# Second attention of a two-block kernel: one scan and differences ahead, masked heads in pairs

## The chip, the cores and the metric

The kernel runs on one core of one Trainium2 chip. The metric is device time in microseconds (us), the median of the runs shown. The engines are named as in the profile: PE is TensorE (PEld its weight loads), DVE is VectorE, ACT is ScalarE, POOL is GpSimd, SP is SyncE.

## The reference

256 tokens of width 1024 pass through two blocks. Each block is an attention part followed by an expert part in which all 16384 experts are computed densely (a product with `u`, a GELU and gate, a product with `v`). What is changed lies in the second block's attention part, which projects the normed tokens with `w_in_2` to seven groups of columns and computes two things from them.

The masked heads (8 heads of width 64, one key block of 256, so only the own block counts):

```python
s_own = einsum('hqd,hkd->hqk', q * hd**-0.5, k) - slopes[:, None, None] * dist
s_own = where(kpos <= tpos, s_own, -inf)
p = softmax(s_own, axis=-1)
o = einsum('hqk,hkd->qhd', p, v)
```

The recurrence (4 heads of width 128), which in closed form over the sequence is

```python
f = lb + (1 - lb) * sigmoid(f_pre);  kk = 1 - f;  cum = cumsum(log(f))
scores[t, s] = sum_d silu(q)[t, d] * exp(cum[t, d] - cum[s, d]) * kk[s, d]   # s <= t
o = scores @ i;  o = rmsnorm(o) * norm_g * silu(g)
```

The two results are concatenated and projected with `w_out_2`, then added to the residual.

## The kernel before, in words

All weights stream through a ring of four slots of 128x1024 (`ring`). SP loads a slot, ACT rounds it to `whi` (`highs_to`, L1206), POOL subtracts to get the rest `wlo` (L560, one instruction per slot), and PE multiplies with three products per pair of tiles, high times high, low times high, high times low (L626 to L628). PE's release of a slot (`slot_used`) lets ACT round the next one, so ACT and POOL must run in step with PE.

The second attention goes through 14 units of 256 columns (`IN2_SLOTS`: fr, fr, qr, qr, qa, ka, va, qa, ka, va, ir, ir, gr, gr). A unit is two ring slots and 48 products. The order of everything around the units is a list written out by `schedule2()`; PE, ACT and DVE each walk the same list in their `attention2()` and do their own share of each item. Every engine executes in order, so an item that waits holds back all that stands behind it in that engine's queue.

The recurrence works on levels: level 0 is the diagonal, level l (1 to 7) takes pairs of positions in blocks of 2^l, level 8 is the part between the two halves of 128. For each level DVE subtracts a column of the running sums from its block (`rec_decay`, L1865), ACT takes two exponentials (L1363, L1364), DVE multiplies them into the queries and keys (`rec_factors`, L1887 and L1888), PE forms the products (`rec_level`, L915) and DVE takes the wanted part of them (`rec_take`, L1875). The running sums come from eight scans of 128 elements, four after unit 2 and four after unit 3 (`rec_sums`, L1857). `LEVEL_AT` puts level l in unit 4 + l. Before the unit come that level's difference, the take of the level below and that level's factors; after it comes the level itself. So difference, exponentials, take and factors of a level all lie within one unit's time.

The masked heads run one at a time through scores on PE (L890, L891: 64 rows of the array), scale, mask and maxima on DVE (L1842 to L1844), exponentials on ACT (L1339), a reciprocal on DVE (L1847), scaling on ACT (L1345), three transposes on PE (L898), a copy on ACT (L1351), the product with the values on PE (L867, L868: 64 columns of the array), and the split of the result on ACT (L1354) and DVE (L1835). `SCORES_AT` gives the unit of each head's scores; its transposes come one unit later and its values two. `ml` and `mpT` hold two heads each, and so does `stat`. Even and odd heads lie in partitions 0 to 63 and 64 to 127, as `rows(h)` says.

The lines quoted here are those whose waits the prediction follows:

```python
pe.wait_ge(g_qk, i)                       # rec_level: factors of the level
pe.wait_ge(g_sc, TT * (i - 1) + t + 1)    # rec_level: the bank was taken
pe.wait_ge(m_prob, TT * (i + 1))          # m_turn: scaled probabilities
eng.wait_ge(g_exp, i)                     # rec_factors: exponentials
```

Of the kernel before, what the change touches and what calls it, by code (L numbers as in the profile page):

```python
# [21 lines left out]
P = 128  # L22
# [9 lines left out]
S = 256  # L32
TT = S // P
# [113 lines left out]
SCORES_AT = (6, 7, 8, 9, 9, 10, 10, 11)  # L147
LEVEL_AT = (4, 5, 6, 7, 8, 9, 10, 11, 12)


def schedule2():

    steps = []
    for s in range(len(IN2_SLOTS)):

        def heads(late):
            return [h for h in range(HEADS) if SCORES_AT[h] + late == s]

        levels = [l for l in range(9) if LEVEL_AT[l] == s]
        for l in levels:  # L160
            steps.append(("rec_decay", l))
        for h in heads(1):
            steps.append(("m_norm", h))
        for l in levels:
            if l:
                steps.extend([("rec_take", l - 1), ("rec_factors", l)])
        if 8 in levels:
            steps.append(("proj_half", s))
            steps.append(("rec_level", 8))
        if s == len(IN2_SLOTS) - 1:  # L170
            steps.append(("rec_norm", 0))
            steps.append(("proj_half", s))
            for h in heads(2):
# [4 lines left out]
        if s in (2, 3):  # L178
            steps.append(("rec_sums", s - 2))
        for l in levels:  # L180
            if l < 8:
                steps.append(("rec_level", l))
        if s == 12:
            steps.append(("rec_values", 0))
        for j in range(2):
            for h in heads(1)[j:j + 1]:
                steps.append(("m_turn", h))
            for h in heads(0)[j:j + 1]:
                steps.append(("m_scores", h))
            if s < len(IN2_SLOTS) - 1:  # L190
                for h in heads(2)[j:j + 1]:
                    steps.append(("m_values", h))
    steps.append(("rec_gate", 0))
    return steps


def block_program(nc, weights, const1, const2, gains, keys_in, x, out):
    with ExitStack() as ctx:
# [144 lines left out]
        rt, at = carve(at, TT, REC_H, P)  # L343
        lbs = work[:, 4608:4608 + 8 * REC_H].rearrange("p (k h) -> p k h", k=8)
# [9 lines left out]
        ones2 = c2[:, o:o + P]  # L354
# [16 lines left out]

        def mstat(h, k, t):

            return stat[:, 4, (h % 2) * 6 + 2 * k + t:(h % 2) * 6 + 2 * k + t + 1]

        def mstat2(h, k):
            return stat[:, 4, (h % 2) * 6 + 2 * k:(h % 2) * 6 + 2 * k + 2]
# [211 lines left out]
        def _(pe):  # L589
# [270 lines left out]
            def head_values(i):  # L860

                pe.wait_ge(m_Tc, i + 1)
                pe.wait_ge(proj_copied, base2 + 1 + i // 4)
                if i >= 2:
                    pe.wait_ge(m_outc, i - 1)
                w, v = mpT[:, i % 2, :], raw2["va"][:, :, i * HD:(i + 1) * HD]
                pe.matmul(ps[rows(i), 2, 0:S], v[:, 0, :], w[:, 0:S], start=True, stop=False, skip_group_check=True)  # L867
                pe.matmul(ps[rows(i), 2, P:S], v[:, 1, :], w[:, S:S + P], start=False, stop=True,  # L868
                          skip_group_check=True).then_inc(m_out, 1)

            def attention2():
                for what, i in schedule2():
# [10 lines left out]
                    elif what == "m_scores":  # L883
                        if i % 4 == 0:
                            pe.wait_ge(col_copied, 6 + i // 2)
                        if i >= 2:
                            pe.wait_ge(m_max, i - 1)
                        q, kT = colT["qa"][rows(i), i // 2, :], colT["ka"][rows(i), i // 2, :]
                        z = Z_BANK[i % 2]
                        pe.matmul(bank(z, 0, P), q[:, 0:P], kT[:, 0:P], start=True, stop=True)  # L890
                        pe.matmul(bank(z, P, P + S), q[:, P:S], kT, start=True, stop=True).then_inc(m_ready, 1)  # L891
                    elif what == "m_turn":
                        pe.wait_ge(m_prob, TT * (i + 1))
                        if i:
                            pe.wait_ge(m_Tc, i)
                        p = ml[:, i % 2, :]
                        for c in range(3):
                            mm = pe.transpose(bank(1, c * P, (c + 1) * P), p[:, c * P:(c + 1) * P], ident[:, :])  # L898
                        mm.then_inc(m_T, 1)
                    elif what == "m_values":  # L900
                        head_values(i)
# [37 lines left out]
                def heads_ready(kc):  # L939
                    pe.wait_ge(m_outc, 2 * kc + 4)  # L940
# [226 lines left out]
        def _(eng):  # L1167
# [139 lines left out]
            def attention2():  # L1307
                base = FIRST_GATE
                for what, i in schedule2():
# [25 lines left out]
                    elif what == "m_scores":  # L1335
                        eng.wait_ge(m_max, i + 1)
                        for t in range(TT):
                            c = slice(0, P) if t == 0 else slice(P, P + S)
                            eng.activation(ml[:, i % 2, c], ml[:, i % 2, c], ACT.Exp, bias=mstat(i, 0, t),  # L1339
                                           accum_out=mstat(i, 1, t)).then_inc(m_exp, 1)  # L1340
                    elif what == "m_norm":
                        eng.wait_ge(m_rec, i + 1)
                        for t in range(TT):
                            c = slice(0, P) if t == 0 else slice(P, P + S)
                            eng.activation(ml[:, i % 2, c], ml[:, i % 2, c], ACT.Copy, scale=mstat(i, 2, t)).then_inc(m_prob, 1)  # L1345
                    elif what == "m_turn":
                        eng.wait_ge(m_T, i + 1)
                        if i >= 2:
                            eng.wait_ge(m_out, i - 1)

                        eng.activation(mpT[:, i % 2, :], bank(1, 0, 384), ACT.Copy).then_inc(m_Tc, 1)  # L1351
                    elif what == "m_values":
                        eng.wait_ge(m_out, i + 1)
                        eng.activation(chi[rows(i), i // 2, :], ps[rows(i), 2, 0:S], ACT.Copy).then_inc(c_hi, 1)  # L1354
# [4 lines left out]
                    elif what == "rec_decay" and i:  # L1359
# [210 lines left out]
        def _(eng):  # L1570
# [251 lines left out]
            def attention2():  # L1822
                base = FIRST_GATE
                R = scale_row.unsqueeze(1).to_broadcast([P, 2, S])
                for what, i in schedule2():
# [7 lines left out]
                    elif what == "m_values":  # L1833
                        eng.wait_ge(c_hi, i + 1)
                        eng.tensor_tensor(clo[rows(i), i // 2, :], ps[rows(i), 2, 0:S], chi[rows(i), i // 2, :].bitcast(F32),  # L1835
                                          ALU.subtract).then_inc(m_outc, 1)
                    elif what == "m_scores":
                        l = ml[:, i % 2, :]
                        eng.wait_ge(m_ready, i + 1)
                        if i >= 2:  # L1840
                            eng.wait_ge(m_T, i - 1)
                        settle(eng.scalar_tensor_tensor(l, bank(Z_BANK[i % 2], 0, 384), HD ** -0.5, c2a[:, i, :], ALU.mult, ALU.add))  # L1842
                        eng.tensor_reduce(mstat(i, 0, 0), l[:, 0:P], AX.X, ALU.max, negate=True)
                        eng.tensor_reduce(mstat(i, 0, 1), l[:, P:P + S], AX.X, ALU.max, negate=True).then_inc(m_max, 1)  # L1844
                    elif what == "m_norm":
                        eng.wait_ge(m_exp, TT * (i + 1))
                        eng.reciprocal(mstat2(i, 2), mstat2(i, 1)).then_inc(m_rec, 1)  # L1847
# [5 lines left out]
                    elif what == "rec_sums":  # L1853
                        eng.wait_ge(g_log, 1)
                        for h in (2 * i, 2 * i + 1):
                            for t in range(TT):
                                tick(eng.tensor_tensor_scan(cum[:, h, t, :], ones2, dlt[:, h, t, :], 0.0, ALU.mult, ALU.add))  # L1857
                        eng.wait_ge(dve_step, steps[0])
                    elif what == "rec_decay" and i:
# [71 lines left out]
            def experts(b):  # L1931
# [132 lines left out]
                if b == 0:  # L2064
# [163 lines left out]
```

## Time and profile before

| What | Value |
| --- | --- |
| Median of 3 runs | 2045.97 us (2045.52 to 2046.14) |
| The profiled execution's own time | 2046.68 us |
| Its span | 2044.9 us |
| DVE, ACT, POOL busy | 61%, 50%, 69% of the span |

The span is the stretch between first and last instruction of the profiled execution; about 1.8 us of its own time lie around it. The second attention's units run from about 1076 to 1201 us of the span. Times on a timeline are counted from the span's start. The duration of a PE instruction includes its way through the array, so in a stream the distance from start to start, not the duration, is what each costs. The line number in a row is that of the kernel before.

### The profile page before, as it was taken

How to read it: one execution, taken by the hardware profiler on the slowest of the kernel's cores; microseconds unless marked ns; L12 is line 12 of the kernel's file. 1: busy time of each engine (PE TensorE's matmuls, PEld its weight loads, DVE VectorE, ACT ScalarE, POOL GpSimd, SP SyncE). 2: the span in 40 equal slices, each digit the busy share in tenths (PEclk: the TensorE clock that was granted, in tenths of full speed). 3: DMA queues.
4: the chain of work that ended last, by engine and by line, in shares of the span. 5: the costliest groups of instructions: out<-in, count | busy, mean ns of one | idle time of the engine just before them, and what ended most of it. 6: DMA issues, size and time to landing. Idle time of an engine off the chain costs nothing.

```text
span 2044.9 us, 39515 instructions
## 1 busy us (share of the span) xinstructions
PE 2022.4 (99%) x14308; PEld 1808.3 (88%) x14308; DVE 1247.5 (61%) x2142; ACT 1031.1 (50%) x1358; POOL 1418.0 (69%) x592
## 2 busy tenths in 40 slices
PE   8999999999999999999999999999999999999998
PEld 8999999999888888888889899999988888888886
DVE  5247469911676799953337537990376789994333
ACT  5557555454555544444446665545445554444443
POOL 6656868888777877754446456888877787775442
PEclk9999999999999999999999999999999999999999
DMA  7433545555545555565555334555555455555553
GB/s 257 154 125 125 174 158 181 178 182 184 173 168 174 175 174 169 170 224 184 192 187 175 104 121 149 185 184 184 176 174 174 168 173 173 174 169 180 185 186 132
DMA packets 97299, 351.46 MB, mean 172 GB/s; under 512 B 12112, under 2 KB 12368, under 8 KB 96848
## 3 DMA queue, kind: packets, MB, share of 16 engines
q1 hardware_dynamic: 96224, 345.40, 50.9%
q10 hardware_dynamic: 1008, 5.13, 0.7%
q8 instruction: 47, 0.77, 0.1%
q14 instruction: 20, 0.16, 0.0%
HBM read 349.44 MB, written 1.05 MB: 171 GB/s over the span
## 4 chain that ended last, share of the span: by engine, by line
PE 96%; DVE 2%; SPq 1%; DMA 0%; issue 0%; ACT 0%; POOL 0%; ACTq 0%; DVEq 0%
PE ps L626 24%; PE ps L628 23%; PE ps L627 23%; PE ps L1027 12%; PE ps L1028 6%; PE ps L1019 3%; PE ps L915 1%; PE ps L1003 1%; DVE act L1857 0%; SPq L536 0%; DMA ring<-in_weights 0%; PE ps L594 0%; DVE act L1865 0%; PE ps L815 0%; PE ps L795 0%
## 5 line engine op out<-in xcount | busy, mean ns | idle before, releaser
L560 POOL TENSOR_TENSOR wlo<-ring,whi 128x1024 fp32r<-128x1024 f32 x584 | 1410.1, 2419 | 594.1 <-ACT whi L1396 455.6
L1396 ACT ACTIVATE whi<-ring 128x1024 fp32r<-128x1024 f32 x536 | 566.4, 1060 | 774.9 <-PE ps L628 588.8
L626 PE MATMUL ps<-whi,shi 128*128 128x512 f32 x1024 | 408.5, 399 | 0.0
L628 PE MATMUL ps<-whi,slo 128*128 128x512 f32 x1024 | 405.9, 396 | 0.0
L627 PE MATMUL ps<-wlo,shi 128*128 128x512 f32 x1024 | 405.9, 396 | 0.0
L626 PE MATMUL ps<-hboth,whi 128*128 128x256 f32 x1392 | 395.7, 284 | 0.0
L627 PE MATMUL ps<-hboth,whi 128*128 128x256 f32 x1392 | 393.8, 283 | 0.0
L628 PE MATMUL ps<-hboth,wlo 128*128 128x256 f32 x1392 | 393.8, 283 | 0.0
L1027 PE MATMUL ps<-hboth,whi 128*128 128x512 f32 x1024 | 359.3, 396 | 0.0
L1028 PE MATMUL ps<-hboth,wlo 128*128 128x256 f32 x1024 | 283.7, 277 | 0.0
L626 PEld LDWEIGHTS ps<-hboth,whi 128*128 128x128 f32 x1392 | 267.1, 192 | 2.2 <-issue 2.0
L627 PEld LDWEIGHTS ps<-hboth,whi 128*128 128x128 f32 x1392 | 267.1, 192 | 0.0
L628 PEld LDWEIGHTS ps<-hboth,wlo 128*128 128x128 f32 x1392 | 267.1, 192 | 0.0
L628 PEld LDWEIGHTS ps<-whi,slo 128*128 128x128 f32 x1024 | 192.8, 188 | 46.8
L626 PEld LDWEIGHTS ps<-whi,shi 128*128 128x128 f32 x1024 | 192.9, 188 | 45.6
L627 PEld LDWEIGHTS ps<-wlo,shi 128*128 128x128 f32 x1024 | 193.0, 188 | 45.4
L1027 PEld LDWEIGHTS ps<-hboth,whi 128*128 128x128 f32 x1024 | 192.1, 188 | 43.0
L2038 DVE TENSOR_TENSOR wlo<-ring,whi 128x1024 fp32r<-128x1024 f32 x64 | 79.4, 1241 | 238.3 <-ACT whi L1396 238.3
L2032 DVE TENSOR_TENSOR slo<-act,shi 128x512 fp32r<-128x512 f32 x128 | 183.8, 1436 | 22.5 <-ACT shi L1460 22.5
L1028 PEld LDWEIGHTS ps<-hboth,wlo 128*128 128x128 f32 x1024 | 192.4, 188 | 0.0
L1994 DVE TENSOR_TENSOR work<-iota,ps 128x1024 f16<-128x1024 f16 x128 | 154.9, 1210 | 0.0
L2004 DVE TENSOR_TENSOR act<-ps,act 128x512 f32 (+1 forms) x128 | 86.9, 682 | 95.2 <-PE ps L1019 95.2
(306 smaller groups left out, 2780.6 us busy)
## 6 DMA issues: line engine op xcount, KB each, us to landing
ring<-in_weights SPq DMA_DIRECT2D x651, 512.0 KB, 3.3
act<-in_const ACTq DMA_DIRECT2D x1, 2372.0 KB, 8.9
act<-in_const SPq DMA_DIRECT2D x1, 2240.0 KB, 12.4
xres<-in_x SPq DMA_DIRECT2D x4, 256.0 KB, 4.5
act<-in_keys ACTq DMA_DIRECT2D x1, 1024.0 KB, 4.8
out<-act ACTq DMA_DIRECT2D x2, 512.0 KB, 2.6
ring<-in_weights SPq DMA_DIRECT2D x2, 256.0 KB, 5.4
act<-in_fgain ACTq DMA_DIRECT2D x1, 512.0 KB, 3.4
```

The lines of the kernel that those rows point to most:

```text
L560: pool.tensor_tensor(wlo[:, j, :], ring[:, j, :], whi[:, j, :].bitcast(F32), ALU.subtract)\
L626: pe.matmul(dst, wide[0], narrow[0], start=start, stop=False, skip_group_check=True)
L627: pe.matmul(dst, wide[0], narrow[1], start=False, stop=False, skip_group_check=True)
L628: return pe.matmul(dst, wide[1], narrow[0], start=False, stop=stop, skip_group_check=True)
L1019: mm = pe.matmul(bank(6 + c, q * HALF, (q + 1) * HALF), hot2[:, c, q, :], hot1[:, c, w, q, :], start=(q + w == 0), stop=(w == 1), skip_gro ...
L1027: pe.matmul(bank(b), whi[:, j, c], hboth[:, :, kc, :], start=kc == 0, stop=False, skip_group_check=True)
L1028: mm = pe.matmul(bank(b, 0, S), wlo[:, j, c], hhi[:, kc, :], start=False, stop=kc == KC - 1, skip_group_check=True)
L1396: eng.activation(whi[:, j, :], ring[:, j, :], ACT.Copy).then_inc(hi_ready[j], 1)
L1994: eng.tensor_tensor(hot2[:, j], iota[:, :].unsqueeze(1).to_broadcast([P, TOK, NKEY]), over(row(1, at), NKEY), ALU.is_equal)
L2004: eng.tensor_tensor(a, bank(6 + j).rearrange("p (q k) -> p k q", q=TOK), a, ALU.mult)\
L2032: eng.tensor_tensor(slo[:, j, :, :], act[:, bass.ds(p * 2, 2), :], shi[:, j, :, :].bitcast(F32), ALU.subtract)\
L2038: eng.tensor_tensor(wlo[:, j, :], ring[:, j, :], whi[:, j, :].bitcast(F32), ALU.subtract)\
```

## The change

The recurrence: one scan of 1024 elements replaces eight of 128. The running sum is cut at each block of 128 by a multiplier `carry`, which is 1 everywhere but 0 at the first element of each block. It is filled by two memsets at the end of the first block's expert part. `rec_decay` moves: level 1's difference and exponentials now follow unit 3, and those of level l + 2 follow level l. `rec_factors` of level l + 1 stand before unit 4 + l. `rec_take` of a level follows the level directly. Level 8 moves from between the halves of unit 12 to before unit 12.

The masked heads go in four pairs, with scores in units 6, 7, 9 and 11, transposes one unit later and values two. PE issues the two heads' scores alternately (rows 0 to 63 and 64 to 127, banks 2 and 3) and their values alternately (both halves of bank 1). The six transposes of a pair fill banks 0 and 1. Each DVE instruction of the softmax handles both heads, as does ACT's copy of the transposes and both splits; ACT's exponentials and scalings stay one per head and token tile. `ml` and `mpT` now hold one pair each, so a pair's scaled scores wait for the transposes of the pair before (`m_T`), and its transposes for that pair's split values (`m_outc`).

```diff
-SCORES_AT = (6, 7, 8, 9, 9, 10, 10, 11)
-LEVEL_AT = (4, 5, 6, 7, 8, 9, 10, 11, 12)
+PAIRS = HEADS // 2
+SCORES_AT = (6, 7, 9, 11)
+PAIR_BANK = 2
+LEVEL_AT = (4, 5, 6, 7, 8, 9, 10, 11)
...
+        level = s - LEVEL_AT[0] if s in LEVEL_AT else None
+        if s == LEVEL_AT[-1] + 1:
+            steps.append(("rec_level", 8))
+        for h in pairs(1):
             steps.append(("m_norm", h))
+        if level is not None:
+            steps.append(("rec_factors", level + 1))
...
         steps.append(("proj", s))
...
+        if s == 2:
+            steps.append(("rec_sums", 0))
+        if s == 3:
+            steps.append(("rec_decay", 1))
+        if s < len(IN2_SLOTS) - 1:
+            for h in pairs(2):
+                steps.append(("m_values", h))
+        if level is not None:
+            steps.append(("rec_level", level))
+            steps.append(("rec_take", level))
         if s == 12:
             steps.append(("rec_values", 0))
+        for h in pairs(1):
+            steps.append(("m_turn", h))
+        for h in pairs(0):
+            steps.append(("m_scores", h))
+        if level is not None and level + 2 <= 8:
+            steps.append(("rec_decay", level + 2))
...
+            def pair_values(i):
                 pe.wait_ge(m_Tc, i + 1)
+                pe.wait_ge(proj_copied, base2 + 1 + i // 2)
+                if i:
+                    pe.wait_ge(m_outc, i)
+                for k, at, q in ((0, slice(0, S), slice(0, S)), (1, slice(S, S + P), slice(P, S))):
+                    for h in range(2):
+                        c = (2 * i + h) * HD
+                        mm = pe.matmul(ps[rows(h), 1, q], raw2["va"][:, k, c:c + HD], mpT[:, h, at], start=k == 0, stop=k == 1,
+                                       skip_group_check=True)
+                mm.then_inc(m_out, 1)
...
+                        for t in range(TT):
+                            for h in range(2):
+                                q, kT = colT["qa"][rows(h), i, :], colT["ka"][rows(h), i, :]
+                                if t == 0:
+                                    mm = pe.matmul(bank(PAIR_BANK + h, 0, P), q[:, 0:P], kT[:, 0:P], start=True, stop=True)
+                                else:
+                                    mm = pe.matmul(bank(PAIR_BANK + h, P, P + S), q[:, P:S], kT, start=True, stop=True)
+                        mm.then_inc(m_ready, 1)
                     elif what == "m_turn":
+                        pe.wait_ge(m_prob, 2 * TT * (i + 1))
                         if i:
                             pe.wait_ge(m_Tc, i)
+                            pe.wait_ge(m_outc, i)
+                        for h in range(2):
+                            for c in range(3):
+                                mm = pe.transpose(bank(h, c * P, (c + 1) * P), ml[:, h, c * P:(c + 1) * P], ident[:, :])
...
+                        eng.activation(mpT, ps[:, 0:2, 0:384], ACT.Copy).then_inc(m_Tc, 1)
...
+                        eng.activation(chi[:, i, :], bank(1, 0, S), ACT.Copy).then_inc(c_hi, 1)
...
+                        if i:
+                            eng.wait_ge(m_T, i)
+                        settle(eng.scalar_tensor_tensor(ml, ps[:, PAIR_BANK:PAIR_BANK + 2, 0:384], HD ** -0.5,
+                                                        c2a[:, 2 * i:2 * i + 2, :], ALU.mult, ALU.add))
+                        eng.tensor_reduce(pair_stat[:, :, 0, 0], ml[:, :, 0:P], AX.X, ALU.max, negate=True)
+                        eng.tensor_reduce(pair_stat[:, :, 0, 1], ml[:, :, P:P + S], AX.X, ALU.max, negate=True).then_inc(m_max, 1)
...
-                        for h in (2 * i, 2 * i + 1):
-                            for t in range(TT):
-                                tick(eng.tensor_tensor_scan(cum[:, h, t, :], ones2, dlt[:, h, t, :], 0.0, ALU.mult, ALU.add))
-                        eng.wait_ge(dve_step, steps[0])
+                        settle(eng.tensor_tensor_scan(cum.rearrange("p h t c -> p (h t c)"), carry, dlt.rearrange("p h t c -> p (h t c)"),
+                                                      0.0, ALU.mult, ALU.add))
...
+                    settle(eng.memset(carry, 1.0))
+                    tick(eng.memset(carry.rearrange("p (n c) -> p n c", c=P)[:, :, 0:1], 0.0))
```

## Rows read from the trace of the kernel before

**Rows 1.** The page, busy time by engine, share of the span, instructions

```profile
PE 2022.4 (99%) x14308; PEld 1808.3 (88%) x14308; DVE 1247.5 (61%) x2142; ACT 1031.1 (50%) x1358; POOL 1418.0 (69%) x592
```

**Rows 2.** Longest waits of PE, 1070 to 1240 us: total us, times, longest

```profile
PE ps L915 <- DVE act L1888: 3.1, 3, 2.2
PE ps L921 <- DVE act L1892: 1.4, 1, 1.4
PE ps L898 <- ACT act L1351: 0.7, 1, 0.7
```

**Rows 3.** Timeline of PE at levels 0, 1, 2 (start, length, idle before)

```profile
1106.68 2.02 PE L915 MATMUL ps<-act 128*128 128x128 f32 x16 [0.60 <-ACT act L1319]
1108.46 0.36 PE L626 MATMUL ps<-hboth,whi 128*128 128x256 f32 x1
...
1116.69 3.00 PE L915 MATMUL ps<-act 128*128 128x128 f32 x16 [2.24 <-DVE act L1888]
1119.34 0.56 PE L626 MATMUL ps<-whi,hboth 128*128 128x256 f32 x1
...
1125.91 1.95 PE L915 MATMUL ps<-act 128*128 128x128 f32 x16
```

**Rows 4.** Busy by stretch (PE, PEld, DVE, ACT, POOL); then the granted PE clock

```profile
1119.30:1121.00 1.70, 1.70 (x10) 1.70 (x10) 1.70 (x3) 1.03 (x2) 0.00 (x0) 0.50 0.57 140
```

**Rows 5.** Timeline of DVE: scans, the second product of level 1's factors

```profile
1102.59 2.55 DVE L1857 TENSOR_TENSOR_SCAN act<-act 128x128 f32<-128x128 f32 x1
...
1105.79 1.36 DVE L1857 TENSOR_TENSOR_SCAN act<-act 128x128 f32<-128x128 f32 x4
...
1113.79 2.85 DVE L1888 TENSOR_TENSOR act<-act 128x512 f32<-128x512 f32 x1
```

**Rows 6.** The differences of the levels: ns least, median, most; first and last start

```profile
L1865 DVE TENSOR_TENSOR act<-act x7: 1206/1217/3245, 1107.8 to 1172.3; 128x1024 f32<-128x1024 f32 x7
```

**Rows 7.** Timeline of POOL, two lows in the same stretch

```profile
1107.56 2.39 POOL L560 TENSOR_TENSOR wlo<-ring,whi 128x1024 fp32r<-128x1024 f32 x1 [2.69 <-ACT whi L1206]
1109.91 3.40 POOL L560 TENSOR_TENSOR wlo<-ring,whi 128x1024 fp32r<-128x1024 f32 x1
```

**Rows 8.** Timeline of PE in and after unit 9 (one head's parts)

```profile
1167.00 0.49 PE L898 MATMUL ps<-ident,act 128*128 128x128 f32 x3
1167.42 0.49 PE L890 MATMUL ps<-act 64*128 64x128 f32 x2
...
1168.27 0.65 PE L867 MATMUL ps<-act 128*64 128x256 f32 x2
...
1169.06 0.55 PE L898 MATMUL ps<-ident,act 128*128 128x128 f32 x3
...
1170.39 0.39 PE L626 MATMUL ps<-whi,hboth 128*128 128x256 f32 x1
...
1176.24 2.00 PE L915 MATMUL ps<-act 128*128 128x128 f32 x16
```

**Rows 9.** Timeline of PE: the values of heads 5 and 6, back to back

```profile
1193.68 0.66 PE L867 MATMUL ps<-act 128*64 128x256 f32 x4
...
1194.49 0.39 PE L626 MATMUL ps<-whi,hboth 128*128 128x256 f32 x1
```

**Rows 10.** Groups of DVE, 1070 to 1205 us, by form (busy, mean ns, idle)

```profile
L1842 DVE SCALAR_TENSOR_TENSOR act<-ps,act 128x384 f32<-128x384 f32 x8 | 4.4, 555 | 21.2 <-PE ps L891 21.1
L1844 DVE TENSOR_REDUCE stat<-act 128x1 f32<-128x256 f32 x8 | 3.3, 408 | 0.0
```

**Rows 11.** Timeline of ACT: highs, exponentials of a head and a level, scaling

```profile
1165.81 2.00 ACT L1206 ACTIVATE whi<-ring 128x1024 fp32r<-128x1024 f32 x2
...
1172.46 0.40 ACT L1339 ACTIVATE act<-act,stat 128x128 f32<-128x128 f32 x1 [1.22 <-DVE stat L1844]
...
1173.59 0.63 ACT L1363 ACTIVATE act<-act 128x512 f32<-128x512 f32 x1
...
1174.65 1.48 ACT L1345 ACTIVATE act<-act,stat 128x128 f32<-128x128 f32 x4
```

More of the change, by code:

```diff
@@ L154, in schedule2, with pairs @@
     for s in range(len(IN2_SLOTS)):
[L156 to L162, printed above, removed]
-            steps.append(("m_norm", h))
[L164 to L169, printed above, removed]
+        def pairs(late):
+            return [h for h in range(PAIRS) if SCORES_AT[h] + late == s]
+        level = s - LEVEL_AT[0] if s in LEVEL_AT else None
+        if s == LEVEL_AT[-1] + 1:
+            steps.append(("rec_level", 8))
+        for h in pairs(1):
+            steps.append(("m_norm", h))
+        if level is not None:
+            steps.append(("rec_factors", level + 1))
         if s == len(IN2_SLOTS) - 1:
@@ L172, in schedule2 @@
             steps.append(("proj_half", s))
-            for h in heads(2):
+            for h in pairs(2):
                 steps.append(("m_values", h))
@@ L177, in schedule2 @@
             steps.append(("rec_prep", 0))
[L178 to L182, printed above, removed]
+        if s == 2:
[3 more added lines that the diff above has]
+        if s < len(IN2_SLOTS) - 1:
+            for h in pairs(2):
+                steps.append(("m_values", h))
+        if level is not None:
+            steps.append(("rec_level", level))
+            steps.append(("rec_take", level))
         if s == 12:
             steps.append(("rec_values", 0))
[L185 to L192, printed above, removed]
+        for h in pairs(1):
[4 more added lines that the diff above has]
+            steps.append(("rec_decay", level + 2))
     steps.append(("rec_gate", 0))
@@ L343, in block_program @@
         rt, at = carve(at, TT, REC_H, P)
+        carry = rt.rearrange("p t h c -> p (t h c)")
         lbs = work[:, 4608:4608 + 8 * REC_H].rearrange("p (k h) -> p k h", k=8)
@@ L883, in attention2 @@
                     elif what == "m_scores":
[L884 to L891, printed above, removed]
+                        if i % 2 == 0:
+                            pe.wait_ge(col_copied, 6 + i)
+                        if i:
+                            pe.wait_ge(m_max, i)
+                        for t in range(TT):
[6 more added lines that the diff above has]
+                        mm.then_inc(m_ready, 1)
                     elif what == "m_turn":
-                        pe.wait_ge(m_prob, TT * (i + 1))
+                        pe.wait_ge(m_prob, 2 * TT * (i + 1))
                         if i:
                             pe.wait_ge(m_Tc, i)
-                        p = ml[:, i % 2, :]
-                        for c in range(3):
-                            mm = pe.transpose(bank(1, c * P, (c + 1) * P), p[:, c * P:(c + 1) * P], ident[:, :])
+                            pe.wait_ge(m_outc, i)
+                        for h in range(2):
+                            for c in range(3):
+                                mm = pe.transpose(bank(h, c * P, (c + 1) * P), ml[:, h, c * P:(c + 1) * P], ident[:, :])
                         mm.then_inc(m_T, 1)
                     elif what == "m_values":
-                        head_values(i)
+                        pair_values(i)
                     elif what == "rec_level":
@@ L939, in heads_ready @@
                 def heads_ready(kc):
-                    pe.wait_ge(m_outc, 2 * kc + 4)
+                    pe.wait_ge(m_outc, kc + 2)
                 def rec_ready(kc):
@@ L1358, in attention2 @@
                                        ACT.Ln).then_inc(g_log, 1)
-                    elif what == "rec_decay" and i:
+                    elif what == "rec_decay":
                         eng.wait_ge(g_dlt, i)
@@ L1834, in attention2 @@
                         eng.wait_ge(c_hi, i + 1)
[L1835 to L1836 removed]
+                        eng.tensor_tensor(clo[:, i, :], bank(1, 0, S), chi[:, i, :].bitcast(F32), ALU.subtract).then_inc(m_outc, 1)
                     elif what == "m_scores":
[L1838 removed]
                         eng.wait_ge(m_ready, i + 1)
[L1840 to L1844, printed above, removed]
+                        if i:
+                            eng.wait_ge(m_T, i)
[3 more added lines that the diff above has]
+                        eng.tensor_reduce(pair_stat[:, :, 0, 1], ml[:, :, P:P + S], AX.X, ALU.max, negate=True).then_inc(m_max, 1)
                     elif what == "m_norm":
[L1846 to L1847 removed]
+                        eng.wait_ge(m_exp, 2 * TT * (i + 1))
+                        eng.reciprocal(pair_stat[:, :, 2, :], pair_stat[:, :, 1, :]).then_inc(m_rec, 1)
                     elif what == "rec_prep":
@@ L1854, in attention2 @@
                         eng.wait_ge(g_log, 1)
-                        for h in (2 * i, 2 * i + 1):
-                            for t in range(TT):
-                                tick(eng.tensor_tensor_scan(cum[:, h, t, :], ones2, dlt[:, h, t, :], 0.0, ALU.mult, ALU.add))
-                        eng.wait_ge(dve_step, steps[0])
-                    elif what == "rec_decay" and i:
+                        settle(eng.tensor_tensor_scan(cum.rearrange("p h t c -> p (h t c)"), carry, dlt.rearrange("p h t c -> p (h t c)"),
+                                                      0.0, ALU.mult, ALU.add))
+                    elif what == "rec_decay":
                         if i >= 2:
```

35 lines of the change are left out of this document (13 added, 22 removed).

## The prediction

> **What bounds the kernel now.** I read the page first: PE is busy for 99% of the span [rows 1], so outside its rare gaps only fewer or cheaper products on PE save time, and what DVE, ACT or POOL save counts only where PE waits for them. Next I read who PE waits for while the second attention runs [rows 2], then the timeline of PE around the longest of those waits, and only then the other queues, to see why the releaser was late.
>
> PE waits four times for a level (0.60 us at level 0, and 3.1 in three waits, 2.24 of them at level 1), 0.7 for a copy of transposed probabilities and 1.4 for level 8's factors [rows 2, 3]. That is 5.8 us in all.
>
> Behind the longest wait the clock falls. The granted clock is 0.50 from 1119.3 to 1121.0, its lower level of 1.2 GHz, after 2.24 us in which PE stood still [rows 3, 4]. Level 1 then takes 2.65 us from start to start against 1.78 for level 0, and unit 6 takes 6.57 against some 5.85 for a unit at full clock (1170.39 to 1176.24) [rows 3, 8]. With 1.8 to 1.9 us for a level at full clock this is 0.8 + 0.7 = 1.5 us.
>
> Why levels 0 and 1 are late is seen on DVE. A scan of 128 elements takes 2.55 us while POOL works and 0.34 (1.36 for four) once POOL stands still [rows 5]. Level 0 needs the last query columns, whose copy stood behind four such scans until 1105.14. Level 1's second factor took 2.85 us for an instruction that costs DVE some 0.7 elsewhere, and one difference took 3.25 instead of 1.2 [rows 5, 6]. POOL pays too: a low took 3.40 instead of 2.39 [rows 7]. So a DVE instruction with two operands in SBUF waits out the low in progress, and the next low is then late by about the DVE instruction's length.
>
> **The recurrence.** One scan replaces eight. Bounds for it: no less than a difference of the same 1024 elements, 1.2 us [rows 6], and no more than eight scans alone, 2.7, plus one low waited out, 2.4 [rows 5, 7]. I take 2.2 of work (128 elements in 0.34, less the fixed part) and one wait of up to 2.4, so it ends near 1099.7, before unit 3 does at about 1100.3. The copy of unit 3 then starts at once, not at 1105.2, and the 0.60 at level 0 goes. The lows behind the scan come up to 2 us later. The nearest is that of unit 4's second slot: started at 1097.4, it would end at 1101.8 (2.4 and 2 more), and PE asks for it near 1103.1. If that cover of 1.3 is gone it costs up to 1 us once.
>
> The Trainium skill (SBUF — State Buffer, its section on the port lock) says that DVE and GpSimd share one port pair, held by whoever starts first for the whole instruction. By that rule alone the one long scan keeps POOL out for all of its 2.2 us; the rows above agree in kind, and the sum stays.
>
> Differences ahead: level l + 2's difference and exponentials now start in unit 4 + l and its product comes two units later. The chain is take, difference (1.2 to 3.25), exponentials (1.06) and factors (1.2, or 2.9 with one low), about 8 us at worst, and PE needs at least 7.7 us a unit. Even level 1, which had the 2.24 wait, gets its factors near 1110 for a product at 1113.5. So all four waits of levels 0 to 7 go: 3.65 us, and the 1.5 us of lost clock with them.
>
> The two memsets of `carry` stand on DVE where it is idle until PE's last expert product; the large one is about 1 us by the scans' element rate or less, priced at nothing, and up to 0.5 us if they outlast that gap.
>
> **The heads on PE.** From start to start one head's transposes cost 0.42, scores 0.85 and values 0.79 us [rows 8]. Heads 5 and 6 already have their values back to back, and both together take 1194.49 - 1193.68 = 0.81 us: the two column halves of the array ran beside each other, though issued one head after the other [rows 9]. So adjacency does it, and alternating adds nothing that I price. Values: 6 x 0.79 + 0.81 = 5.5 before, 4 x 0.81 = 3.2 after, a gain of 2.3. For scores no row shows two row halves at once. Bounds for a pair are 0.85 and 1.70; I take 0.85 because the values are the nearest row, a gain of 8 x 0.85 - 4 x 0.85 = 3.4, or nothing. Transposes: six in 0.8 against 2 x 0.42, gain 0.1 to 0.3. Sum 6.0, bounds 2.4 and 6.0.
>
> **What is late next.** With one buffer for a pair, PE's transposes wait for a longer chain. In its queue order, for a pair: scale and mask 1.0 on DVE (two heads of 0.555, one fixed part saved), maxima 1.1 (0.41 for 256 elements, more for 512) [rows 10]; then the difference, 1.2 to 3.25, which stands ahead of the reciprocal [rows 6]; the pair's four exponentials (1.1 a head) run beside it; then on ACT the level's exponentials 1.06 and four scalings 1.48 [rows 11]. I put the difference at 2.5 where lows run. That makes 7.1.
> - Transposes of pair 0 (unit 7): DVE is still at level 2's take for 1.4, so 8.5 against 5.85 + 1.9 on PE: 0.7 us of waiting.
> - Pair 1 (unit 8): its transposes also need pair 0's split values. On ACT these stand behind the scalings and two highs (2.0), then a copy on ACT and one on DVE, about 1.5 with the hand-overs (an estimate from 0.555 for 384 elements). 7.1 + 2.0 + 1.5 = 10.6 against 5.85 + 0.8 + 1.9 = 8.5: 2.1 us. Behind these transposes PE has the scores and unit 9, and everybody waits with it.
> - Pair 2 (unit 10): 1.0 us, since split values and a take stand ahead of its scaling. Pair 3 has unit 12 and the recurrence's products ahead of it and does not wait.
> - Level 8: the take of level 7 stands behind pair 2's split, which stands behind an eviction (0.9), two highs (2.0) and a copy on ACT: about 4.5 after the values, against 1.9 + 0.85 on PE, of which the eviction hides some. I take 1.3, in place of the 1.4 of before.
> - The output projection asks for pair 3's split values, which stand behind the recurrence's norm on ACT: 1.0 us.
>
> New waits 6.1 us, bounds 0 and about 10. The Trainium skill (TensorEngine Tiling (Array Packing), PSUM Bottleneck) warns that tiling speeds up TensorE but not the evacuation of PSUM. By that rule taken whole all 6.0 us of the products' gain would come back as waits, where my list gives back 3.8 at the transposes; the net would then be 5.0 in place of the one below.
>
> **Sum.** Gains 5.8 + 1.5 + 6.0 = 13.3, new waits 6.1, net 7.2 us. From the profiled execution's 2046.68 that gives 2039.5; the median is 0.7 lower, so I say 2038.8. The rest of the kernel starts that much earlier and is unchanged, with PE as its bound.
>
> **Rivals.**
> - *The row halves do not overlap.* PE pays 3.4 more, but 1.7 to 3.1 of it fall into the waits above, since PE arrives later where it would have waited. Net gain 4 to 7, so 2039 to 2042. For it: no row shows it. Against it: the column halves [rows 9].
> - *The new waits do not come.* ACT and DVE have idle time in every unit, and if the differences meet no low the chain is 1.3 shorter. Gain 10 to 13, 2033 to 2036.
> - *The clock falls again.* A wait of 2.1 us at pair 1 is nearly as long as the one that went with the drop of before. Price 1.5, so about 2040.5.
> - *The pair chain meets a low at each step, and the kernel is slower.* Place: DVE in units 6 to 10. If the difference and both factors of every unit wait out a low, each adds 2 us, so 4 more on three chains and 12 in all: waits of 18 against gains of 13.3, 2050.7. It decides from 7.2 more us of waiting. For it: levels 1's 2.85 and 3.25 [rows 5, 6]. Against it: the median difference is 1.217, and two lows of 2.4 fill little over half of a unit [rows 6, 7].
> - *The change is no change*: gains and waits cancel within 4 us.
>
> **Chances.** 0.60 for the forecast, with the clock's fall as part of it; 0.16 for row halves that do not overlap; 0.10 for no new waits; 0.09 for near cancellation; 0.05 for the slower case. This measurement tells about 0.2%, 4.1 us, from no change. Faster by more than that: 0.60 + 0.13 + 0.10, the second since a part of it ends above 2041.9, and a little of the near cases, 0.84. Within: 0.12. Slower: 0.04. The range from 2034 to 2042.5 takes in the waits from 1 to 10 us.
>
> **What would show it.** One scan near 1095 to 1100, its length 2 to 4.5 us. Levels 0 to 7 start without a wait on DVE, and the granted clock stays at 1.00 near 1119. L890's and L891's successors take some 0.85 us a pair, the values 0.81. The waits of PE are now at the transposes, released by ACT, the longest in unit 8. The stage ends near 1194, not 1201. The prediction is wrong if scores take 1.7 us a pair, if levels still wait, or if the waits at the transposes sum to less than 1 or more than 8 us.

## The result and the profile after

The changed kernel takes 2034.18 us (median of 6 runs, 2033.74 to 2034.36) against 2045.6 us for the kernel before (6 runs, 2044.01 to 2046.14). The ratio is 0.9946, interval 0.9934 to 0.9958: 11.4 us faster, where 7.2 was forecast. 2034.18 lies only 0.2 us inside the lower edge of the range, 2034 to 2042.5.

From the turn of the scale ahead of unit 1 to the first transposes of the output projection, the profiled execution took 121.5 us before (1082.67 to 1204.20) and takes 110.0 after (1081.30 to 1191.30). So the second attention holds the whole difference of the medians. The two profiled spans differ by 1.3 us more, which arises before unit 1; the single times of the kernel before scatter by as much.

The longest waits of PE from 1070 to 1240 us, as in [rows 2]:

```profile
PE ps L905 <- DVE clo L1843: 1.7, 1, 1.7
PE ps L905 <- ACT act L1354: 0.7, 1, 0.7
PE ps L928 <- DVE act L1880: 0.6, 1, 0.6
```

No level up to 7 waits any more (L922 is now their line). Two pairs' transposes (L905) and level 8 (L928) do, 3.0 us in all against 5.8. PE's timeline at level 1, and the granted clock of that stretch, answer to [rows 3, 4]:

```profile
1112.09 1.95 PE L922 MATMUL ps<-act 128*128 128x128 f32 x16
1113.79 0.36 PE L626 MATMUL ps<-whi,hboth 128*128 128x256 f32 x1
```

```profile
1112.00:1114.00 2.00, 2.00 (x21) 2.00 (x20) 2.00 (x2) 1.62 (x2) 1.95 (x2) 1.00 0.24 53
```

Level 1 costs 1.70 us instead of 2.65, at a granted clock of 1.00. DVE's timeline shows the one scan, level 1's difference and factors, as in [rows 5]:

```profile
1093.84 4.35 DVE L1862 TENSOR_TENSOR_SCAN act<-act 128x1024 f32<-128x1024 f32 x1
1099.07 0.69 DVE L1839 TENSOR_TENSOR act<-ps,work 128x512 f32<-128x512 f32 x1 [0.87 <-PE ps L628]
1099.67 1.80 DVE L1870 TENSOR_TENSOR act<-act 128x1024 f32<-128x1024 f32 x1
1103.23 1.07 DVE L1892 TENSOR_TENSOR act<-act 128x512 f32<-128x512 f32 x1 [1.76 <-ACT act L1372]
1104.23 2.85 DVE L1893 TENSOR_TENSOR act<-act 128x512 f32<-128x512 f32 x1
```

The scan's 4.35 us contain the wait for a low: one ran on POOL from 1093.64 to 1096.04, and 2.15 us of scan follow it. The next low took 4.39 us instead of 2.40. The scan ends 0.87 us before PE has unit 3 ready, so the copy no longer stands behind it. Level 1's factors end near 1107.1, for a product at 1112.1. On PE, one pair's scores and another's values answer to [rows 8, 9]:

```profile
1121.50 0.49 PE L894 MATMUL ps<-act 64*128 64x128 f32 x4
1121.83 0.60 PE L896 MATMUL ps<-act 64*128 64x256 f32 x4
1122.36 0.39 PE L626 MATMUL ps<-hboth,whi 128*128 128x256 f32 x1
...
1138.42 0.87 PE L869 MATMUL ps<-act 128*64 128x256 f32 x8
1139.22 2.05 PE L922 MATMUL ps<-act 128*128 128x128 f32 x16
1142.97 0.85 PE L905 MATMUL ps<-ident,act 128*128 128x128 f32 x6 [1.70 <-DVE clo L1843]
```

Start to start, a pair's scores take 0.86 us, what one head's took before, and its values 0.80. The last row is the longest wait left. ACT and DVE show what made it:

```profile
1140.11 1.99 ACT L1213 ACTIVATE whi<-ring 128x1024 fp32r<-128x1024 f32 x2
1142.01 0.36 ACT L1362 ACTIVATE chi<-ps 128x256 fp32r<-128x256 f32 x1
```

```profile
1134.52 3.12 DVE L1870 TENSOR_TENSOR act<-act 128x1024 f32<-128x1024 f32 x1
...
1142.40 0.42 DVE L1843 TENSOR_TENSOR clo<-ps,chi 128x256 fp32r<-128x256 f32 x1 [1.65 <-ACT chi L1362]
```

Pair 0's values left PE at 1139.2, but their copy on ACT (L1362) began at 1142.0, behind two highs, and DVE's half of the split (L1843) behind that copy. Ahead of the highs stood the scalings, which had waited for the level's exponentials, and these for the difference of 3.12 us (L1870), which waited out a low. e6 and e7 tell which of the two mattered.

### The profile page after: what moved, and what is told of

Same layout as the page of the kernel before. It is cut to its first block, busy times and chain, and to the rows that moved or that the text cites. A ratio compares the mean times of both kernels' runs of the same rounds, so it can differ in the third digit from the quotient of the medians.

```text
span 2032.1 us, 39467 instructions
## 1 busy us (share of the span) xinstructions
PE 2013.0 (99%) x14308; PEld 1802.6 (89%) x14308; DVE 1244.8 (61%) x2117; ACT 1027.2 (51%) x1350; POOL 1420.6 (70%) x592
## 4 chain that ended last, share of the span: by engine, by line
PE 97%; DVE 1%; ACT 1%; DMA 0%; issue 0%; POOL 0%; SPq 0%; POOLq 0%; ACTq 0%; DVEq 0%
PE ps L626 24%; PE ps L628 24%; PE ps L627 24%; PE ps L1034 12%; PE ps L1035 6%; PE ps L1026 3%; PE ps L1010 1%; PE ps L922 0%; DMA ring<-in_weights 0%; PE ps L594 0%; PE ps L795 0%; PE ps L815 0%; PE ps L824 0%; POOL wlo L569 0%; ACT whi L1213 0%
```

## The experiments

The stretch named below runs, as above, from the turn of the scale to the first transposes of the output projection: 121.5 us before, 110.0 changed. The comparisons were made beside runs of the kernel before, whose medians were 2045.5 for the first four, 2044.7 for the next four and 2044.5 for e9. The times of the kernel before fall in two clusters, below 2045 and above it (e10 to e12 say why), and a median depends on how many of each it holds. The median of the faster cluster alone moved by 0.3 us at most between the sets, so differences against the changed kernel's 2034.18 are good to about that.

**e1: the recurrence's part alone.** The scan, `carry`, differences, factors, takes and level 8 as changed; the single heads with their code of before.

```diff
-SCORES_AT = (6, 7, 9, 11)
+SCORES_AT = (6, 7, 8, 9, 9, 10, 10, 11)
```

> The recurrence's part alone: one scan, differences two units ahead, takes and level 8 as in the changed kernel; the eight heads run singly as before. Theory (waits and the clock went with the recurrence, products with the pairs): the level waits of 3.65 us and the clock's fall of 1.5 are gone, the 0.7 for a copy and level 8's wait (1.4) may stay or shrink, PE's products are unchanged: 4.5 to 6.5 us faster than before, about 2040. No wait on DVE at levels 0 to 7, granted clock 1.00 near level 1. Rival (the levels wait because DVE is busy with the single heads): the waits at levels 3 and 6 (0.28 and 0.53) stay and new ones come, gain under 4 us.

Measured: 2037.81 us (5 runs), ratio 0.9963 (0.9949 to 0.9977), 7.7 us faster; the stretch takes 113.4. One wait is left:

```profile
PE ps L899 <- ACT act L1352: 0.7, 1, 0.7
```

Level 8's wait went too, and the clock did not fall. The rival fell: levels 3 and 6 do not wait, with the single heads in place. The gain lies above the expected 4.5 to 6.5. Waits (5.1) and clock (1.5) make 6.6 of the stretch's 8.1 us. The rest is what PE pays beside a wait: a unit's 48 products took 6.00 to 6.02 us ahead of a wait and 5.85 without one, 1.0 us in all. The eight levels together cost another 0.5 less than before at full clock.

**e2: the heads' part alone.** Eight scans, and differences, takes and factors ahead of the level's unit, level 8 within unit 12, as before.

```diff
-LEVEL_AT = (4, 5, 6, 7, 8, 9, 10, 11)
+LEVEL_AT = (4, 5, 6, 7, 8, 9, 10, 11, 12)
```

> The heads' part alone: pairs on half arrays as in the changed kernel; the recurrence with eight scans, differences in the level's own unit and level 8 between the halves, as before. Theory: products save 6.6 us (scores 3.4, values 2.3, transposes 0.9), the level waits of 3.65 and the clock's fall stay, and the transposes of a pair wait some 1 to 2 us: 3.5 to 6 us faster than before, about 2041. With the other part alone it sums to the whole within 1.5 us. Rival (the two parts need each other): the pair's longer softmax stands between take and factors on DVE, levels wait more, gain under 2 us, and the two parts alone sum to less than 9 of the 11.4.

Measured: 2043.88 us (10 runs, 2042.69 to 2045.15), ratio 0.9993 (0.9983 to 1.0002). That is 1.7 us in the medians, and an interval that takes in no change. Its times fall in two clusters too, five around 2043.0 and five around 2044.8; against the clusters of the kernel before beside it (2044.4 and 2045.9) it is 1.3 and 1.2 us faster. The theory's 3.5 to 6 fell. PE's products were as cheap as in the changed kernel, but:

```profile
PE ps L923 <- DVE act L1896: 4.7, 3, 2.2
PE ps L929 <- DVE act L1900: 3.5, 1, 3.5
PE ps L923 <- ACT act L1327: 0.6, 1, 0.6
PE ps L906 <- DVE clo L1844: 0.4, 1, 0.4
```

These are 9.2 us of waits instead of 5.8. A pair's mask and maxima stand on DVE ahead of a level's take and factors, and with the difference in the level's own unit there is no room for both. Level 8 alone waits 3.5 us, and the clock falls twice, behind that wait and behind the one of 2.23, at a price of about 1.5 us each:

```profile
1115.60:1118.40 2.80, 2.80 (x15) 2.80 (x16) 2.80 (x2) 0.00 (x0) 2.16 (x1) 0.61 0.50 187
1179.80:1183.50 3.70, 0.26 (x3) 0.05 (x1) 3.26 (x6) 3.70 (x13) 0.18 (x1) 1.00 0.56 210
1184.00:1187.00 3.00, 3.00 (x18) 3.00 (x18) 0.00 (x0) 2.19 (x3) 2.37 (x1) 0.58 0.00 0
```

The parts alone sum to 9.4 of the 11.4 us, between the theory's "within 1.5" and the rival's "less than 9"; the rival's mechanism and its gain under 2 us are what was measured. The pairs are worth 1.7 without the advance and 2037.81 - 2034.18 = 3.6 with it.

**e3: a pair's products one head after the other.**

```diff
-                for k, at, q in (...):
-                    for h in range(2):
+                for h in range(2):
+                    for k, at, q in (...):
...
-                        for t in range(TT):
-                            for h in range(2):
+                        for h in range(2):
+                            for t in range(TT):
```

> The changed kernel, but PE issues all of the first head's scores and then the second's, and the same for the values. Theory (adjacency is enough, as in the values of heads 5 and 6 before): a pair's scores stay at 0.86 us and its values at 0.80, time as the changed kernel's within 0.5 us. Rival (products start strictly in program order, so only the seam between the heads overlaps): scores about 1.3 to 1.5 and values 1.2 to 1.4 a pair, 8 such groups cost 3.5 to 4.5 us, of which the waits at transposes hide up to 2.

Measured: 2034.38 us (4 runs, 2034.23 to 2034.74) against 2034.18. Scores and values keep their 0.86 and 0.81 us:

```profile
1121.82 0.50 PE L894 MATMUL ps<-act 64*128 64x128 f32 x4
1122.15 0.61 PE L896 MATMUL ps<-act 64*128 64x256 f32 x4
1122.68 0.39 PE L626 MATMUL ps<-hboth,whi 128*128 128x256 f32 x1
```

In the program the first head's L896 now stands ahead of the second head's L894 (each shows as two records), and yet the rows, in order of start, show all four L894 records first, the two heads' 0.01 us apart. So both heads run side by side though one was issued behind the other. Alternating brings nothing beside adjacency.

The Trainium skill (TensorE: Matmul & The Clock Gate, the section on packing small matmuls) says that matmuls start and end strictly in program order. By that rule only the seam of the two heads would overlap, and e3 would have cost PE 3.5 us or more, of which waits could hide 2. The rows above differ from it, for products on different halves of the array, and the measurement decides.

**e4: the eight scans back.**

```diff
-        if s == 2:
-            steps.append(("rec_sums", 0))
+        if s in (2, 3):
+            steps.append(("rec_sums", s - 2))
```

> The changed kernel with the scans as before, four after unit 2 and four after unit 3, level 1's difference behind them. Theory (scans each wait out a low, the copy of unit 3 stands behind four): level 0 waits 0.6 us again, and level 1's factors come near the end of unit 5, so level 1 waits 0 to 1.5: 0.6 to 2.5 us slower than the changed kernel. Rival (the scan was the whole cause of the early waits, and the advance of the differences adds nothing): level 1 waits 2.2 us again with the clock's fall, 4.3 us slower.

Measured: 2036.96 us (5 runs), 2.8 slower than the changed kernel; the stretch takes 112.5. Level 0 waits 0.6 again and level 1 not at all. DVE is about 2.5 us late, and the delay comes out at pair 0's transposes:

```profile
PE ps L906 <- ACT act L1355: 2.4, 1, 2.4
PE ps L929 <- DVE act L1883: 0.6, 1, 0.6
PE ps L923 <- ACT act L1327: 0.6, 1, 0.6
```

Behind these 2.36 us the granted clock fell to 0.50 until 1137.6, and pair 1's wait shrank to 0.13. The waits sum to 3.7 us against the changed kernel's 3.0, so more than half of the 2.8 us is the clock: pair 0's transposes and pair 1's scores took 1.23 and 1.59 us instead of 0.80 and 0.86, and unit 8 took 6.34 instead of 5.94. The size is just above the theory's upper end, and it came by another way. The rival (level 1 waits 2.2 again) fell: with differences ahead, level 1 does not need the fast scan.

**e5: the one scan and nothing else, in the kernel before.** The edit is the scan and the memsets of the diff.

> The kernel before with one scan in place of eight, and nothing else; each difference still in its level's own unit. Theory (the early waits are the scans' waiting on lows, the later ones the short time within one unit): level 0's 0.6 us goes, level 1's 2.24 shrinks to 0 to 1.0 since its difference still stands behind unit 4's copy, the clock does not fall, and 0.28, 0.53, 0.7 and 1.4 stay: 3.3 to 4.3 us faster than before, about 2041.7. Rival (level 1 is late by its place, not by the scans): its wait stays near 2.2 with the clock's fall, gain 0.6 only.

Measured: 2042.62 us (11 runs, 2042.31 to 2042.95) against 2044.66, ratio 0.9989 (0.998 to 0.9998): 2.0 us faster. Level 0 does not wait, level 1 still waits 1.6, and the clock did not fall:

```profile
PE ps L916 <- DVE act L1887: 2.5, 3, 1.6
PE ps L922 <- DVE act L1891: 1.4, 1, 1.4
PE ps L899 <- ACT act L1352: 0.7, 1, 0.7
```

The gain depends on which of the two clusters of the kernel before it is held against: 1.5 us on the faster, 3.0 on the slower. Level 0's wait, the clock and the four later waits came as the theory said, but level 1's wait lies between theory and rival: the scans made 0.6 of its 2.24, its place the rest. The advance of the differences, with level 8's move and the earlier takes, is worth 2042.62 - 2037.81 = 4.8 us.

**e6: the split's copy ahead of the highs, on ACT alone.**

```diff
+                order = schedule2()
+                for n in range(1, len(order)):
+                    if order[n][0] == "m_values" and order[n - 1][0] == "proj":
+                        order[n - 1:n + 1] = [order[n], order[n - 1]]
```

> The changed kernel, but on ACT alone the copy of a pair's split values goes ahead of the unit's eviction and two highs. Theory (pair 1's transposes and level 8 wait for DVE's split, which waits behind two highs of 2.0 us on ACT): the wait of 1.70 falls to under 0.3, level 8's 0.65 goes, pair 0's 0.66 stays: 2.0 to 2.4 us faster than the changed kernel, about 2032. Rival (highs that come later starve the ring, or the scaling is late anyway): a new wait of PE on lows of 1 us or more, or the wait at pair 1 stays above 1.0: gain 0 to 1, or a loss.

Measured: 2032.06 us (5 runs, 2031.69 to 2032.35), 2.1 faster than the changed kernel. Pair 1's 1.70 and level 8's 0.65 are gone, and PE waits for no low, as the theory had it. So the split's place behind the highs was the cause of both. One wait above 0.1 us is left:

```profile
PE ps L905 <- ACT act L1358: 0.7, 1, 0.7
```

**e7: each difference from level 2 on behind the next unit's reciprocal,** ahead of its factors.

```diff
-        if level is not None and level + 2 <= 8:
-            steps.append(("rec_decay", level + 2))
...
+            if level:
+                steps.append(("rec_decay", level + 1))
```

> The changed kernel, but each difference from level 2 on stands behind the next unit's reciprocal, one place later and still a unit ahead of its product. Theory (pair 0's scaling waits behind the level's exponentials, which wait for a difference that waits out a low): pair 0's 0.66 goes, pair 1's 1.70 shrinks by 0 to 0.7, levels still do not wait, level 8's 0.65 stays: 0.6 to 1.4 us faster than the changed kernel, about 2033.2. Rival (the later difference makes factors late): levels 1 or 2 wait 0.5 us or more and the gain is gone or turns into up to 2 us of loss.

Measured: 2033.29 us (5 runs, 2032.86 to 2035.12), 0.9 faster. Pair 0's 0.66 is gone and level 8's 0.64 stays, as expected, but pair 1's wait grew to 1.93 where 1.0 to 1.7 was expected: PE comes to it 0.9 us earlier, counted from unit 1, and the split only 0.7. One of the five times, 2035.12, lies 1.8 us above their median; it was not profiled, and whether the clock fell in it is open.

**e8: e6 and e7 together.**

> Both edits together, the split's copy first on ACT and the differences behind the reciprocal. Theory: none of the three waits is left, 2.6 to 3.2 us faster than the changed kernel, about 2031.3, and PE has no wait above 0.2 us between units 1 and 13. Rival (something else is late next, the highs or level 2's factors): some wait of 0.5 to 2 us appears, and both together are no better than the better of the two alone.

Measured: 2032.6 us (5 runs, 2031.78 to 2032.89), no better than e6 alone. The rival held, but what is late is the split itself, and not the highs or level 2's factors that it named:

```profile
1137.66 1.19 DVE L1874 TENSOR_TENSOR act<-act 128x1024 f32<-128x1024 f32 x1
1140.35 0.69 DVE L1896 TENSOR_TENSOR act<-act 128x512 f32<-128x512 f32 x1 [1.49 <-ACT act L1376]
...
1142.16 0.41 DVE L1847 TENSOR_TENSOR clo<-ps,chi 128x256 fp32r<-128x256 f32 x1
```

ACT had the copy ready at 1140.6, but DVE split only behind the later difference's exponentials, the factors and unit 8's copy. Pair 1's transposes wait 1.57 for it.

**e9: e6, and only level 4's difference moved** (`LATE = 4`), behind the reciprocal of pair 0.

```diff
+        if level == LATE - 1:
+            steps.append(("rec_decay", LATE))
...
+        if level is not None and level + 2 <= 8 and level + 2 != LATE:
```

> The changed kernel with the split's copy first on ACT, and of the differences only level 4's behind the next reciprocal (pair 0's, the one place where a difference held up a scaling that PE waited for). Theory (with all differences moved, pair 1's split stood behind later factors on DVE; with one moved it does not): the waits at pairs 0 and 1 are both under 0.2 us, no wait of PE above 0.2 in the second attention, about 0.7 us faster than with the split first alone, 2031.4. Rival (unit 7's shift on DVE moves pair 1's maxima back and its wait returns): 0.5 to 1.6 us of waiting at pair 1 and no gain over 2032.1.

Measured: 2031.02 us (5 runs, 2030.87 to 2031.64), ratio to the kernel before 0.9934 (0.992 to 0.9947). PE has no wait above 0.07 us in the second attention, and the stretch takes 107.0. The theory held. This version beats both kernels: it is 3.2 us faster than the changed one, where the three waits it removes had summed to 3.0.

**e10, e11, e12: the kernel before, looked at again.**

> The kernel before, unchanged, one more profiled execution. Its times fall in two clusters, 2043.8 to 2044.7 and 2045.5 to 2046.4. Theory (the clock's fall after the wait at level 1 comes in about half of the executions and costs the 1.5 us between the clusters): an execution near 2044.2 shows the same waits and a granted clock of 1.00 at level 1, one near 2046 shows 0.50 for 4 us. Rival (the clusters come from elsewhere, such as the load of the first slots): the clock falls in both, or in neither.

> The kernel before once more, to have executions of both clusters: by the theory the one of the slower cluster has the fall of the granted clock at level 1 and the one of the faster has not; by the rival the two do not differ there.

> The kernel before a third time, since both executions above were of the slower cluster (2045.8) and both had the clock's fall. Theory: if this one is near 2044.2, its granted clock stays at 1.00 at level 1 behind the same wait of 2.24 us; if it is near 2046, the fall is there again. Rival: near 2044.2 with the fall, or near 2046 without it.

Measured: 2045.77, 2045.86 and 2044.60 us. All three show the waits of before, 2.23 or 2.24 us at level 1 among them. In e10 and e11 the clock fell behind it, in e12 it did not. Stretches of e10, then of e12:

```profile
1116.00:1118.00 2.00, 2.00 (x14) 2.00 (x15) 2.00 (x2) 0.00 (x0) 2.00 (x1) 0.72 0.71 254
1118.00:1120.00 2.00, 2.00 (x12) 2.00 (x10) 2.00 (x3) 0.87 (x2) 0.02 (x1) 0.50 0.40 119
1120.00:1122.00 2.00, 2.00 (x17) 2.00 (x17) 1.67 (x3) 0.39 (x1) 0.00 (x0) 0.92 0.41 160
```

```profile
1116.00:1118.00 2.00, 1.90 (x17) 1.91 (x18) 2.00 (x3) 0.00 (x0) 2.00 (x1) 1.00 0.60 211
1118.00:1120.00 2.00, 2.00 (x19) 2.00 (x18) 2.00 (x3) 0.62 (x2) 0.26 (x1) 1.00 0.43 133
```

The stretch takes 121.5 us in e10 and 120.0 in e12. So the two clusters of the kernel before are the same program with and without one fall of the clock, as far as four profiled executions show it. The mean granted clocks of the unprofiled ones agree: over the 40 executions of the kernel before that were timed beside the others, it is 0.999 in 13 of the 22 below 2045 us and in none of the 18 above. Why the same wait brings the fall in one execution and not in another is not shown. The changed kernel is about 10 us faster than the one and 11.5 faster than the other.

## Why the prediction came out so

The sign, the places and most terms were right; the gain was forecast too small, mainly because one term, the new waits, was twice too large. The time itself was nearly missed: 2034.18 is 4.6 us below the 2038.8 forecast and lies in the band of the rival without new waits (2033 to 2036). Step by step:

- *Level waits gone* (5.8 us with the two single waits; levels 3.65 of it): right. Levels 0 to 7 wait for nothing. The scan ended within 0.2 us of the place forecast, counted from unit 1. The low behind it was 2.0 us late, as forecast, and PE did not wait for it.
- *The clock*: 1.5 us, right for the profiled execution, and e12 shows that executions without the fall exist, with the 1.5 us missing from the stretch. Against these the term is zero, which the prediction did not know; four of the six times of the kernel before in the result are of the slower cluster. It also gave the clock a chance to fall after a wait of 2.1 us. The wait was 1.70 and it did not.
- *Scores* 3.4 and *values* 2.3: right, 8 x 0.85 against 4 x 0.86, and 5.6 against 4 x 0.80. The open bound for the row halves closed at its good end. That adjacency is enough was read from one pair of rows [rows 9]; e3 shows it for both kinds.
- *Transposes*: forecast 0.1 to 0.3 us, measured 0.9 (3.45 for eight heads, 2.55 for four pairs). A group of six took 0.57 to 0.60, except pair 0's at 0.80.
- *New waits*: forecast 6.1 us, measured 3.0. This is the term that was mis-sized. Pair 0: 0.7 forecast, 0.66 measured. Pair 1: 2.1 and 1.70, released by DVE's split behind two highs, as described; copy and split took 1.0 and not 1.5. Pair 2: 1.0 and none. Level 8: 1.3 and 0.65; the eviction of 0.9 on ACT ended with the values (1168.2, 1168.1), where the prediction let it hide in part. Output projection: 1.0 and none.
- Pair 2 was put too late in part because the difference was priced at 2.5 us in every unit. Behind unit 9 it took 1.22, because the last low was just ending (POOL's pair ran from 1151.46 to 1156.21, the difference began at 1156.12):

```profile
1156.12 1.22 DVE L1870 TENSOR_TENSOR act<-act 128x1024 f32<-128x1024 f32 x1
```

  At 2.5 it would have ended near 1158.6, and the level's exponentials, which began at 1158.02, would have come 0.6 us later. That estimate from the rows covers 0.6 of the 1.0. The rest is that the mask began 1.1 us after the scores, where the forecast's sum implies about 1.6. The scalings ended at 1160.5 and PE came at 1160.8, so there was little to spare.
- The output projection did not wait, since pair 3's split ended at 1188.2 and PE asks for it six products into the projection, near 1189.1. The split does stand behind the recurrence's norm on ACT, as the prediction says, but ACT was through with that at 1186.4.

The sum of what is measured: waits 2.8, clock 1.5, products 6.6 give 10.9 of the stretch's 11.5 us. The remaining 0.6 lies in what PE pays beside its waits, which the prediction did not price: the 48 products of a unit take 0.15 us more ahead of a wait (6.00 to 6.02 against 5.83 to 5.97), and all units' products together took 0.8 us less than before at full clock. The levels gave 0.2 to 0.3 of it back: six of the eight cost 1.8 to 2.05 us each, among them the two whose next item waits.

The rivals: row halves overlap, so that one fell; the slower case fell with the level waits. The new waits came at half the size, so the outcome lies between the forecast and the rival without them, and that rival's reason, differences that meet no low, holds for level 7's (1.22 us) and not for those of levels 4 to 6 (3.05 to 3.20). Of the signs named, the waits at transposes sum to 2.4 us (1 to 8 allowed), but the longest was released by DVE's split and not by ACT. What the prediction did not see is how the two parts depend on each other. The pairs alone are hardly worth having (e2), since their longer work on DVE needs the room that the advance makes.

## What to carry to other kernels

Before making PE's work cheaper, make room in the queues of the engines that feed it: the same pairing gained 1.7 us (1.2 to 1.3 cluster against cluster) where differences and factors had one unit's time and 3.6 where they had two. Where the chain of a wait is known, move the one item that holds it up and no more. Moving all the differences (e8) brought the wait back at another instruction; moving one (e9) did not. Where the times of one program fall in two clusters, profile an execution of each and compare the granted clock: here that told them apart.

## What the hardware showed beyond what was expected

- Products on different halves of the array overlap fully in the records, by rows or by columns, also when all of one half's instructions stand ahead of the other's: 0.86 us for two heads' scores and 0.81 for two heads' values, in either order of issue.
- PE stood still for 2.23, 2.24, 2.36 and 3.54 us in five executions (before, e2, e4, e10, e11), and the granted clock fell to 0.50 for between 3 and 4 us each time. It stayed at 1.00 after 1.60, 1.70 and 1.93 us (e5, changed, e7), and in e12 after 2.24 us. The shortest wait with a fall and the longest without overlap, so the wait's length alone does not decide it. The price at level 1 was 1.5 us.
- A DVE instruction with two operands in SBUF and 1024 elements took 1.2 us alone and 3.05 to 3.25 when a low was running, and one scan of 1024 elements took 4.35 with such a wait, against eight scans of up to 2.55 each.
